# The scan input's projection: six of its eight contraction slices in upper and lower parts, made pair by pair in borrowed homes

## The reference, cut to what matters

```python
z = x @ w_in[i]                                   # (512, 1024) @ (1024, 1792)
u_pool, q, k, v, u_ssm = jnp.split(z, splits, axis=-1)   # u_ssm: the last 384 columns
...
y_ssm = s5_mixer(u_ssm, ...)                      # needs abar, bbar and their powers, then a scan
```

## Time and profile before

| what | value |
|---|---|
| median of 3 runs | 464.48 us (463.85 to 464.62) |
| the profiled execution's own time | 464.56 us |
| its span, first to last instruction | 462.8 us |
| mean granted TensorE clock | 0.995 |
| instructions | 5294, of them PE 1885 matmuls |

### The profile page before, as it was taken

One profiled execution on the slowest core, in us unless ns is written; L12 is line 12 of the kernel. 1 busy time (PEld: TensorE's weight loads), 2 busy tenths in 40 slices (PEclk: granted clock), 3 DMA queues, 4 the chain that ended last, 5 costly groups with the idle time before them and its releaser, 6 DMA issues.

```text
span 462.8 us, 5294 instructions
## 1 busy us (share of the span) xinstructions
PE 441.7 (95%) x1885; PEld 288.9 (62%) x1885; DVE 323.0 (70%) x502; ACT 219.8 (47%) x360; POOL 114.0 (25%) x146
## 2 busy tenths in 40 slices
PE   5999999999999999999999999999999999999881
PEld 2444564487676544446587766777777777777640
DVE  3699959885434676776484255867878777789677
ACT  3111361051987900213311046778888778789422
POOL 7880042470066200000005420022111221111200
PEclk9999999999999999999999999999999999999997
DMA  8994023236983991110820139999999999840673
GB/s 269 382 378 143 0 40 86 48 94 167 410 356 108 347 396 57 45 47 0 317 93 1 8 103 390 403 423 420 412 393 371 374 363 370 331 190 20 240 186 136
DMA packets 36904, 103.14 MB, mean 223 GB/s; under 512 B 16012, under 2 KB 22076, under 8 KB 30096
## 3 DMA queue, kind: packets, MB, share of 16 engines
q1 hardware_dynamic: 27584, 91.68, 52.6%
q0 software_dynamic: 5600, 9.44, 6.6%
q10 hardware_dynamic: 3696, 1.71, 1.4%
HBM read 95.39 MB, written 17.86 MB: 245 GB/s over the span
## 4 chain that ended last, share of the span: by engine, by line
PE 87%; DVE 5%; ACT 4%; DMA 2%; issue 1%; SPq 0%; DVEq 0%
PE bank L925 12%; PE bank L1089 12%; PE bank L1262 9%; PE bank L1234 6%; PE bank L932 5%; PE bank L1239 4%; PE bank L1243 4%; PE bank L1247 4%; PE bank L1161 3%; PE bank L1163 3%; PE bank L1162 3%; PE bank L1175 3%; PE bank L1218 3%; PE bank L941 2%; PE bank L950 2%; PE bank L1004 1%
## 5 line engine op out<-in xcount | busy, mean ns | idle before, releaser
L1089 PE MATMUL bank<-region_b,region_e 128*128 128x512 f32 x128 | 58.3, 601 | 0.6 <-DVE region_f L1592 0.6
L925 PE MATMUL bank<-region_e,region_a 128*128 128x512 f32 x128 | 55.9, 595 | 0.0
L925 PEld LDWEIGHTS bank<-region_e,region_a 128*128 128x128 f32 x128 | 24.1, 190 | 29.4 <-issue 29.2
L1089 PEld LDWEIGHTS bank<-region_b,region_e 128*128 128x128 f32 x128 | 23.2, 190 | 25.0 <-issue 23.6
L1239 PE MATMUL bank<-gate_up_upper,tokens_upper 128*128 128x512 f32 x96 | 36.2, 459 | 0.0
L557 POOL DMA_INDIRECT slot_scratch<-region_h,slot_i x8 | 8.4, 1055 | 92.8 <-issue 92.8
L1746 DVE TENSOR_TENSOR gate_up_lower<-region_a,gate_up_upper 128x1024 fp32r<-128x1024 f32 x24 | 28.0, 1221 | 2.7 <-ACT gate_up_upper L844 2.7
L1243 PE MATMUL bank<-gate_up_upper,tokens_lower 128*128 128x512 f32 x96 | 29.8, 392 | 0.0
L570 POOL DMA_INDIRECT expert_scratch<-region_g,region_h x8 | 10.0, 1253 | 80.1 <-ACT region_g L871 80.1
L932 PE MATMUL bank<-region_e,region_a 128*128 128x512 f32 x48 | 23.8, 660 | 4.9 <-DMA region_a<-in_w_in 4.9
L1161 PE MATMUL bank<-ple_gate_upper,hidden_upper 128*128 128x512 f32 x64 | 26.5, 415 | 0.0
(11 more groups left out here) (331 smaller groups left out, 1012.3 us busy)
## 6 DMA issues: line engine op xcount, KB each, us to landing
region_a<-in_w_exp_gate SPq DMA_DIRECT2D x8, 1024.0 KB, 8.5
region_a<-in_w_exp_up SPq DMA_DIRECT2D x8, 1024.0 KB, 17.8
region_a<-in_w_exp_down SPq DMA_DIRECT2D x8, 1024.0 KB, 17.7
region_a<-in_w_in SPq DMA_DIRECT2D x3, 1536.0 KB, 17.2
region_b<-in_w_out SPq DMA_DIRECT2D x1, 4096.0 KB, 14.6
expert_scratch<-zero_scratch SPq DMA_DIRECT2D x8, 512.0 KB, 13.4
region_b<-in_w_exp_gate SPq DMA_DIRECT2D x4, 1024.0 KB, 9.2
region_b<-in_w_exp_up SPq DMA_DIRECT2D x4, 1024.0 KB, 17.5
```

The source lines that it names most:

```text
L925: last = mm(bank[bank_i][:], w[:, k, m * P:(m + 1) * P], xT[:, k, :], start=(k == 0), stop=(k == KD - 1))
L1089: last = mm(bank[WO_AT[half][group]][:], hdT[:, k, t * P:(t + 1) * P], w_o[:, k, half * 512:half * 512 + 512], start=(i == 0), stop=(i == ...
```

## The change

Slices 0 and 1 of the projection stay float32 matmuls. Slices 2 to 7 are taken in three pairs. For a pair, ACT copies both slices of x and both slices of the weights into fp32r tensors (`ux_hi`, `uw_hi`), DVE subtracts these from the originals into `ux_lo` and `uw_lo`, and PE makes three groups of six fp32r matmuls. The new tensors lie in homes that are used later by others: `ux_hi` in `region_g` (q and k), `uw_hi` and `ux_lo` in `region_c` (`bxT` and `bx`), `uw_lo` in place of the weights' own slices. Because `ux_lo` lies where `bx` is written, DVE waits for `pe_u` = 3 ahead of the `cmul` into `bx`. The overflow loop, which runs only when an expert has more tokens than its slot, uses fewer semaphores.

```diff
+        ux_hi = over("input_upper", 6 * T, G0)
+        uw_hi = over("state_weights_upper", 6 * SSM_W, C0 + 4 * 3072)
+        ux_lo = over("input_lower", 6 * T, C0)
+        uw_lo = over("state_weights_lower", 6 * SSM_W, A0 + 4 * 2 * SSM_W)
...
             a.activation(sinh[:], angr[:], ACT.Sin, scale=0.5).then_inc(S["trig"], 1)
+
+            for i in range(3):
+                if i < 2:
+                    ac.wait_ge(S[f"x_in{2 + i}"], 32)
+                k = slice(2 + 2 * i, 4 + 2 * i)
+                a.activation(ux_hi[:, 2 * i * T:2 * (i + 1) * T].rearrange("p (k t) -> p k t", k=2), xT[:, k, :], ACT.Copy).then_inc(S["uhi_set"], 1)
+                a.activation(uw_hi[:, 2 * i * SSM_W:2 * (i + 1) * SSM_W].rearrange("p (k n) -> p k n", k=2), w_ssm[:, k, :],
+                             ACT.Copy).then_inc(S["uhi_set"], 1)
 
             ac.wait_ge(S["small_in"], 32)
...
-            for k in range(KD):
-                if k in FIRST_K:
-                    pe.wait_ge(S[f"x_in{FIRST_K.index(k)}"], 32)
+            for k in range(2):
+                pe.wait_ge(S[f"x_in{k}"], 32)
                 for m in range(3):
-                    last = mm(bank[m][:], w_ssm[:, k, m * P:(m + 1) * P], xT[:, k, :], start=(k == 0), stop=(k == KD - 1))
-                    if k == KD - 1:
+                    mm(bank[m][:], w_ssm[:, k, m * P:(m + 1) * P], xT[:, k, :], start=(k == 0), stop=False)
+
+            def u_term(i, w, x, stop=False):
+                for m in range(3):
+                    for k in (2 * i, 2 * i + 1):
+                        last = mm(bank[m][:], w[:, k * SSM_W + m * P:k * SSM_W + (m + 1) * P], x[:, k * T:(k + 1) * T],
+                                  start=False, stop=(stop and k == 5))
+                    if stop:
                         last.then_inc(S["pe_u"], 1)
+
+            for i in range(3):
+                pe.wait_ge(S["uhi_set"], 2 * i + 2)
+                u_term(i, uw_hi, ux_hi)
+                pe.wait_ge(S["ulo_set"], 2 * i + 1)
+                u_term(i, uw_hi, ux_lo)
+                pe.wait_ge(S["ulo_set"], 2 * i + 2)
+                u_term(i, uw_lo, ux_hi, i == 2)
...
             link(v.reciprocal(c1, c1))
+
+            def u_lower(i):
+                k = slice(2 + 2 * i, 4 + 2 * i)
+                dv.wait_ge(S["uhi_set"], 2 * i + 1)
+                tt(ux_lo[:, 2 * i * T:2 * (i + 1) * T].rearrange("p (k t) -> p k t", k=2), xT[:, k, :],
+                   ux_hi[:, 2 * i * T:2 * (i + 1) * T].rearrange("p (k t) -> p k t", k=2), ALU.subtract).then_inc(S["ulo_set"], 1)
+                dv.wait_ge(S["uhi_set"], 2 * i + 2)
+                tt(uw_lo[:, 2 * i * SSM_W:2 * (i + 1) * SSM_W].rearrange("p (k n) -> p k n", k=2), w_ssm[:, k, :],
+                   uw_hi[:, 2 * i * SSM_W:2 * (i + 1) * SSM_W].rearrange("p (k n) -> p k n", k=2), ALU.subtract).then_inc(S["ulo_set"], 1)
+
+            u_lower(0)
+            u_lower(1)
+            u_lower(2)
             link(tt(c2, nr, are, ALU.mult))
...
             t4 = tmp[:, 0:Q * CH * GD].rearrange("p (q j h) -> p q j h", q=Q, j=CH)
+            dv.wait_ge(S["pe_u"], 3)
```

More of the change, by code:

```diff
@@ L284, in trunk @@
         S = {n: sem(n) for n in (
-            "x_in0 x_in1 x_in2 x_in3 wqk_in wv_in wup_in small_in par_in rb_in gp_in wglu_in rc_in "
+            "uhi_set ulo_set x_in0 x_in1 x_in2 x_in3 wqk_in wv_in wup_in small_in par_in rb_in gp_in wglu_in rc_in "
             "wo_in wpg_in wpp_in ln_in xh_in "
@@ L295, in trunk @@
             "pe_aT aT_evac pe_dn ye_evac yh_set yl_set y2_in "
-            "o_col o_in o_hg o_t o_te o_gu o_si o_a o_at o_ae o_dn o_ye o_out o_round aT_hi dn_hi_set dn_lo_set "
+            "o_col o_in o_hg o_act o_pe o_a o_ye o_out o_round aT_hi dn_hi_set dn_lo_set "
             "y_in0 y_in1 y_in2 y_in3 o_acc z2_ready ln2_in one_added var2_done o_dve out_st").split()}
@@ L896, in _ @@
                     with ac.If(o < n_over):
-                        ac.wait_ge(S["o_t"], o + 1)
+                        ac.wait_ge(S["o_pe"], 4 * o + 1)
                         for u in range(2):
                             a.activation(hgT[:, 0, 4 * u:4 * u + 4, :], bank[B_TOK[u]][:].rearrange("p (k s) -> p k s", k=4),
[L900 to L904, removed]
+                                         ACT.Copy).then_inc(S["o_act"], 1)
+                        ac.wait_ge(S["o_pe"], 4 * o + 2)
+                        a.activation(act_e[:, 0, 0, :], bank[B_GU[0]][:, 0:DE], ACT.Silu).then_inc(S["o_act"], 1)
+                        ac.wait_ge(S["o_pe"], 4 * o + 3)
+                        a.activation(act_e[:, 0, 2, :], bank[B_ACT[0]][:, 0:DE], ACT.Copy).then_inc(S["o_act"], 1)
             def deviation(t):
@@ L1321, in _ @@
                         pe.wait_ge(S["o_hg"], 16 * (o + 1))
-                        turn_tokens(0).then_inc(S["o_t"], 1)
-                        pe.wait_ge(S["o_te"], 2 * (o + 1))
+                        turn_tokens(0).then_inc(S["o_pe"], 1)
+                        pe.wait_ge(S["o_act"], 4 * o + 2)
                         pe.wait_ge(S["o_in"], 48 * (o + 1))
-                        gate_up(0, 0).then_inc(S["o_gu"], 1)
+                        gate_up(0, 0).then_inc(S["o_pe"], 1)
                         pe.wait_ge(S["o_a"], o + 1)
-                        turn_act(0).then_inc(S["o_at"], 1)
-                        pe.wait_ge(S["o_ae"], o + 1)
-                        down(0, 0).then_inc(S["o_dn"], 1)
+                        turn_act(0).then_inc(S["o_pe"], 1)
+                        pe.wait_ge(S["o_act"], 4 * o + 4)
+                        down(0, 0).then_inc(S["o_pe"], 1)
                         pe.wait_ge(S["o_ye"], 2 * o + 2)
@@ L1801, in _ @@
                         v.tensor_copy(cur_t[:, 1:2], inv_i[:, bass.ds(o + NE, 1), 0]).then_inc(S["o_col"], 1)
-                        dv.wait_ge(S["o_si"], o + 1)
+                        dv.wait_ge(S["o_act"], 4 * o + 3)
                         tt(act_e[:, 0, 1, :], act_e[:, 0, 0, :], bank[B_GU[0]][:, DE:2 * DE], ALU.mult).then_inc(S["o_a"], 1)
-                        dv.wait_ge(S["o_dn"], o + 1)
+                        dv.wait_ge(S["o_pe"], 4 * o + 4)
                         ts(y_e[0][:, 0:512], bank[B_DN[0]][:], cur_w, None, ALU.mult).then_inc(S["o_ye"], 1)
```

## The result

The changed kernel takes 472.39 us, median of 6 runs (471.88 to 474.53); the kernel before takes 464.28 us beside it (6 runs, 463.85 to 465.63). The ratio is 1.0178, with a 95% interval of 1.0155 to 1.0202: about 8.1 us slower. The prediction was 467.7 us, with a range to 470.7 us. The sign was right, the time lies outside of the range, and the loss is two and a half times the 3.1 us that were forecast.

A forecast was written before the change was run, and what follows sets the result against it. PE bound the kernel, DVE only 1.6 us ahead at kern. PE gains 1.9 us at `qk(0)`, but DVE, 4.7 us late, starts kern 3.1 us late: 464.56 + 3.1 = 467.7 us, range 465.8 to 470.7 us.

The forecast's parts named there:

- PE's part: Scan projection: fp32r matmuls save 3.1 us taken alone; it ends near 26.1 us, `qk(0)` gains 1.9 us, held by a load.
- The mechanism on DVE and POOL: Ahead of kern: subtractions hold POOL too, DVE is 4.7 us late at `s_read`, kern starts 3.1 us late.
- rival A: POOL's table beside DVE: POOL gets clear ahead, DVE 0.3 us late, kern 1.3 us early, 463.3 us; chance 0.07.
- B: POOL's table beside DVE: POOL keeps its old times, DVE 1.8 us late, kern 0.2 us late, 464.8 us; chance 0.07.
- The eight small instructions that follow (to L1425) take 15.30 - 13.38 = 1.9 us.: DVE behind the subtractions: they end at 23.3 us, so the first `cmul` starts 4.9 us late.
- high bound of 5.2: DVE's lateness at `bx_ready` and `s_read`: 5.2 us if POOL stretches the subtractions themselves.
- C, the clock falls at kern: PE's idle time ahead of kern lowers its clock: up to 3.0 us more, 470.7 us; chance 0.12.
- So 3.1 us go through to the end.: Behind kern: everything hangs on its start, so its 3.1 us of lateness reach the end, giving 467.7 us.
- No load there is tied to a fixed time: Behind kern: each load is released by an event that hangs on kern, supporting the 3.1 us going through.

The follow-up runs named there:

- experiment 1: Changed kernel with ACT's copies and DVE's subtractions kept but unused, PE multiplying in float32 as before: 469.97 us, ratio 1.0129 to the kernel before.
- experiment 3: Changed kernel with POOL's 192- and 384-column table instructions put behind DVE's small `cmul`s, bias mask moved in front: 466.84 us, ratio 1.0060 to the kernel before.
- experiment 7: Changed kernel with one pair only (slices 2 and 3) in parts, slices 4 to 7 float32 again: 464.52 us, ratio 0.9997 to the kernel before.
- 14 dummies: Kernel before with fourteen unused float32 matmuls more on PE ahead of kern's waits: 477.73 us, ratio 1.0285 to the kernel before.
- experiment 9: Late table alone: kernel before with POOL's 192- and 384-column table instructions put behind DVE's powers, projection all float32: 464.67 us, ratio 0.9998.
- two pairs: Changed kernel with slices 2 to 5 in parts, 6 and 7 float32, POOL's large table instructions behind DVE's powers: 464.54 us, ratio 1.0005 to the kernel before.
- experiment 2: Changed kernel with three unused float32 matmuls more on PE ahead of kern's waits: 471.19 us, ratio 1.0146 to the kernel before.
- experiment 8: Changed kernel with one pair only (slices 2 and 3) and POOL's large table instructions behind DVE's powers: 464.48 us, ratio 0.9996 to the kernel before.

## Why the prediction was wrong, point by point

**PE's part was right.** The forecast had the first twelve records through at about 13.0 us. In the kernel before the thirteenth starts at 12.6 us; in the changed kernel the twelve were through at 11.46 us, and PE's next group waited for ACT until 12.83 us. The projection was through at 26.2 us (forecast 26.1), `qk(0)` started at 26.74 (26.7), held by the load, and from 19.23 us on the groups of six fp32r matmuls followed each other in 1.36 us, against the 1.37 us of the earlier trace rows.

**The mechanism on DVE and POOL was right.** DVE's `s_read` sets kern, POOL is held by the subtractions, its copy comes at 36.9 us (forecast "near 37"), and neither rival A nor B came true: DVE's small instructions still met POOL's large ones. Experiments 1 and 3 show both halves of it: the work of ACT and DVE alone makes 5.7 of the 8.1 us, and taking POOL's large instructions out of DVE's way removes 5.5 us.

**Step that was mis-sized: "The eight small instructions that follow (to L1425) take 15.30 - 13.38 = 1.9 us."** They took 2.9 us. I had worked out that the subtractions push POOL's 48-column instructions back by 4 to 5 us, and did not ask which of POOL's instructions the eight then meet: the last 48- and the first 96-column ones, of 0.30 to 0.39 us, where before they met those of 12 and 24 columns, of 0.22 to 0.31 us. The wide `cmul`, opposite the 192-column ones, took 5.9 us instead of some 5, and the narrow ones behind it gave 1.3 us back. DVE was 5.4 us late at `s_read`, where 4.7 was taken, outside even the high bound of 5.2, and kern 3.97 us late instead of 3.1.

**Step that failed: the clock.** "C, the clock falls at kern" was given 0.12, because a wait of 1.8 us late in the kernel leaves it up and its rise at the start takes a while. That the start is a rise of the clock was my estimate, and so was the bound of 3.0 us that rests on it; no run shows it: the weight loads come 0.86 us apart for 6 us and then 0.43 us, but the granted clock reads 1.00 over both stretches. At kern it fell after 3.09 us, to 0.50, in the changed kernel and in experiment 1, and the price was 1.67 us in the changed kernel, under the bound of 3.0. The forecast had a wait of 2.9 us in it, and the row that I argued from has one of 1.8 us: no row of the kernel before showed what a wait as long as the forecast's own does. And little more than those 1.8 us was enough in experiment 7, where the clock fell to 0.54 behind a wait of 1.90 us.

**Step that failed: "So 3.1 us go through to the end."** Up to expert 0 they do, to 0.1 us. Behind it they do not: 1.8 us more. Of these 1.32 us (3.86 - 2.54) lie in the gap between two read-backs, and 0.5 us between expert 0 and the first of them. With 14 dummies a pure delay of 12 us costs some 1.4 us more than itself (0.5 to 2.0), with no fp32r work at all, so such a delay does not go through unchanged. "No load there is tied to a fixed time" was argued from what releases each transfer, and said nothing of how long it takes: 6.59 us for the second read-back before, 8.07 us in the changed kernel. Why it lands later in some kernels stays open, and with it whether the 1.8 us belong to the change: the profiled execution of the late table alone is 1.6 us longer behind expert 0 than the one before, with no delay of PE. The transfers with which POOL accumulates rows (L595 before) are issued 0.5 us behind the first addition and could compete with the second read-back, but they are in both groups; this was not tried.

**Not foreseen: 0.4 us outside of the span.** It is there in every kernel with three pairs (2.1 to 2.2 us), about half of it with two pairs (2.0), and absent with one pair (1.8) and with dummies (1.7 to 1.8), though the semaphores of the overflow loop are the same with one pair as with three. So it is not these semaphores; what it is was not found.

**The range.** Its high end added the clock's bound to the forecast, but no lateness of DVE beyond it, and nothing behind kern. The three misses, 0.9, 1.7 and 1.8 us, and the 0.4 us have one sign; each of them alone would have stayed within it.

## What to carry to other kernels

Where two engines take turns, as DVE and POOL do here, a delay of one is not a shift of its list: ask which of the other's instructions each of yours meets at its new time, the smallest ones too (here DVE's 36 columns took 0.20 us opposite POOL's 12 and 24 columns and 0.41 us opposite its 96), and price it with those. A wait that you introduce on PE can have a price beyond its length: behind the 3.09 us here the granted clock was 0.50, and kern and the products took 1.67 us more. And where two lists are nearly level, look at both before you take from the one and give to the other: PE could gain no more than the 1.6 us that DVE was ahead, and of DVE's 5.4 us of lateness all beyond them came through to kern. One pair, which fits into DVE's idle time, costs nothing and gains nothing that can be measured, and three pairs cost 8 us.

## What the runs showed of the hardware

The granted clock stayed at 1.00 behind waits of 1.82 us (before, ahead of L1355) and 1.86 us (experiment 3, ahead of kern), and over 1.62 and 0.61 us with 1.07 us of matmuls between (the changed kernel). It had fallen to 0.50 behind 3.09 us (the changed kernel and experiment 1), to 0.50 from 55.5 to 57 us behind 2.28 and 0.61 us with 1.06 us of matmuls between (experiment 2), to means of 0.65, 0.57 and 0.61 over some 3 us behind 2.59, 2.51 and 2.53 us near the end of experiments 3, 8 and 9, and to 0.54 behind 1.90 us near the end of experiment 7. So 1.82 and 1.86 us are waits that did no harm in these executions, and not a length that is safe.

At the start the full rate came between 7.9 and 10.9 us in different executions with the same first matmuls (10.88 in the earlier trace rows, 7.9 in the changed kernel): weight loads 0.86 us apart up to there and 0.43 us apart behind it. The granted clock reads 1.00 on both sides (before: 4.8 to 10.8 and 10.8 to 13.0 us), so it does not show what holds the matmuls back at the start. The time at which the full rate comes moves `qk(0)` and kern by up to 0.9 us in the float32 kernels (kern at 60.6 to 61.5 us), as much as a small change is worth.

DVE and POOL opposite each other: POOL's 48 columns take 0.3 us beside DVE's short instructions and 0.87 to 1.15 us opposite a subtraction; DVE's 36 columns take 0.20 us beside POOL's 12 and 24 columns, 0.41 opposite 96 and 0.98 opposite 384. The engine with the longer instruction pays as well, but less than the other's instruction takes: in experiment 3 DVE's 1536 columns go from 1.76 us to between 1.96 and 2.00 us, and 3072 columns from 3.36 to 3.88 us with one of POOL's 192 or 384 columns beside each (384 take 0.85 us beside DVE's short ones).
